# Decoder block on one core: the stage between the out products and the routed experts, by token tiles

## The reference, cut to what matters

```python
x = x + merged @ w_out[i]
h2 = rmsnorm(x, g_ffn[i]).reshape(T, D)
idx, wts = route(h2, w_router[i], router_bias[i])        # sigmoid scores, best 4 of 8 groups, best 8 of 64 experts
moe = routed_experts(h2, idx, wts, w_exp_gate[i], w_exp_up[i], w_exp_down[i]) \
    + swiglu(h2, w_sh_gate[i], w_sh_up[i], w_sh_down[i])  # shared expert, 256 wide
x = x + moe.reshape(B, S, D)
ple_gate = jax.nn.sigmoid(rmsnorm(x, g_ple[i]) @ w_ple_gate[i])
x = x + ple_gate * rmsnorm(p[i] @ w_ple_proj[i], g_ple_post[i])
```

## Time and profile before

| | us |
|---|---|
| median of three runs | 1049.26 (1048.88 to 1050.40) |
| the profiled execution | 1053.37 |
| its span, first to last instruction | 1051.5 |
| TensorE busy | 970.8 (92%) |
| VectorE busy | 290.6 (28%) |
| ScalarE busy | 161.7 (15%) |
| mean granted clock of TensorE | 0.968 of 2.4 GHz |
| first routed up product begins | 397.0 |

### The profile page before, as it was taken

The page is one execution under the profiler, slowest core; times in us unless marked ns, Lnnn a source line. Parts: engine busy times, 40 slices in busy tenths (PEclk is TensorE's granted clock), DMA queues, the critical chain, the costliest instruction groups (busy, mean ns, idle before and its releaser), DMA issues.

```text
span 1051.5 us, 14841 instructions
## 1 busy us (share of the span) xinstructions
PE 970.8 (92%) x6019; PEld 412.9 (39%) x6019; DVE 290.6 (28%) x672; ACT 161.7 (15%) x301; POOL 167.7 (16%) x324
## 2 busy tenths in 40 slices
PE   6999999999999899999999999999987889786598
PEld 4554554444344344333433333333332333232243
DVE  3322642003211564333333111111110101010677
ACT  2002230150000101111111111111110211120021
POOL 4245000000000010222222222222212121201000
PEclk9999999999999899999999999999998989998699
DMA  9351211221231917999999999999999999997972
GB/s 337 123 160 42 79 41 49 71 80 40 75 137 41 373 47 287 368 402 416 410 402 407 400 397 418 417 405 365 423 421 421 421 420 419 420 397 288 374 264 80
DMA packets 74787, 292.79 MB, mean 278 GB/s; under 512 B 8196, under 2 KB 26272, under 8 KB 49760
## 3 DMA queue, kind: packets, MB, share of 16 engines
q1 hardware_dynamic: 61968, 255.90, 62.0%
q0 software_dynamic: 12176, 33.86, 8.3%
q10 hardware_dynamic: 576, 2.10, 0.5%
HBM read 275.57 MB, written 25.69 MB: 286 GB/s over the span
## 4 chain that ended last, share of the span: by engine, by line
PE 74%; DMA 20%; DVE 2%; SPq 1%; issue 1%; ACT 1%; POOL 0%; POOLq 0%; DVEq 0%
PE ps L1713 22%; DMA ring<-in_w_exp_up 18%; PE ps L1441 11%; PE ps L1741 8%; PE ps L1826 5%; PE ps L1543 5%; PE ps L1362 3%; PE ps L1425 3%; PE ps L1385 3%; PE ps L1528 3%; PE ps L1526 3%; PE ps L1589 2%; PE ps L1391 1%; PE ps L1574 1%; PE ps L1724 1%
## 5 line engine op out<-in xcount | busy, mean ns | idle before, releaser
L1713 PE MATMUL ps<-ring,gates 128*32 128x512 f32 x2624 | 301.9, 614 | 33.9 <-DMA ring<-in_w_exp_up 32.4
L1713 PEld LDWEIGHTS ps<-ring,gates 128*32 128x32 f32 x2624 | 93.2, 113 | 236.8 <-issue 235.0
L1741 PE MATMUL ps<-ring,poolbuf 128*32 128x512 f32 x1312 | 149.3, 595 | 1.7 <-ACT actT L776 0.9
L1212 DVE COPY poolbuf<-ps 128x256 f32<-128x256 f32 x41 | 17.4, 424 | 416.3 <-PE ps L1724 416.3
L1441 PE MATMUL ps<-actT,ring 128*128 128x512 f32 x256 | 112.3, 596 | 0.0
L603 POOL TENSOR_TENSOR tickets<-cst 128x1 f32<-128x1 f32 x79 | 14.8, 188 | 397.4 <-ACT actT L776 391.8
L1741 PEld LDWEIGHTS ps<-ring,poolbuf 128*32 128x32 f32 x1312 | 38.9, 110 | 88.6 <-issue 87.3
L1441 PEld LDWEIGHTS ps<-actT,ring 128*128 128x128 f32 x256 | 48.0, 190 | 59.5 <-issue 59.4
L776 ACT ACTIVATE actT<-ps,qT 128x1024 f32<-128x1024 f32 x41 | 45.6, 1113 | 149.2 <-PE ps L1741 149.2
L1362 PE MATMUL ps<-cst,rows 128*128 128x128 f32 x392 | 54.9, 288 | 11.3 <-DMA cst<-in_constants 9.0
L768 ACT ACTIVATE poolbuf<-ps 128x256 f32<-128x256 f32 x41 | 15.7, 384 | 286.0 <-PE ps L1713 286.0
(11 more groups left out here) (227 smaller groups left out, 830.8 us busy)
## 6 DMA issues: line engine op xcount, KB each, us to landing
ring<-in_w_exp_gate SPq DMA_DIRECT2D x64, 1024.0 KB, 13.7
ring<-in_w_exp_up SPq DMA_DIRECT2D x64, 1024.0 KB, 16.7
ring<-in_w_exp_down SPq DMA_DIRECT2D x64, 1024.0 KB, 16.8
ring<-accumulator SPq DMA_DIRECT2D x16, 1024.0 KB, 14.1
ring<-in_w_gate SPq DMA_DIRECT2D x8, 1024.0 KB, 11.5
ring<-in_w_in SPq DMA_DIRECT2D x5, 1024.0 KB, 12.7
ring<-in_w_out SPq DMA_DIRECT2D x4, 1024.0 KB, 5.2
ring<-in_w_ple_gate SPq DMA_DIRECT2D x4, 1024.0 KB, 16.2
```

What stands on the lines that cost most here:

```text
L1713: last = mm(bank(2 + k)[part, :], hgT[k][:, q, part], pair_view(EXPERT_SLOT[js[c]])[:, q], start=(q == 0), stop=(q == KD - 1))
L1741: last = mm(bank(6 + half)[part, :], eactT[r % 2][:, q, part], w[:, q, half * 512:(half + 1) * 512], start=(q == 0), stop=(q == 1))
```

## The change

All stages from the residual addition to the lists are done tile by tile and placed between the out products.

- `out_proj` is called by halves and quarters; for tile 0, half 0, product k waits only for `merged_ready` k+1.
- The rows are no longer scaled before they are transposed. `second_T(i, half)` transposes `xrow` itself, and VectorE multiplies by g_ffn while it copies (g_ffn as a column comes with `vecs`, one more small load on GpSimd's queue). Rows for DRAM are made by `gained_rows` (VectorE, times g_ffn) and a scaled copy on ScalarE. The square of the last tile goes to PSUM.
- The router runs per tile, eight products of 64 columns with the tile as the stationary operand; the reciprocal root is a scale of the sigmoid. The copy and the four transposes of the logits are gone. The router's, and the shared gate's and up's, weights are loaded with channels in the other order (rows of 256 B and 1 KiB instead of 2 KiB and 8 KiB per partition).
- `select(i)` makes the whole selection of a tile, and `rank(i)` its ranks. Sorting uses transposes of the masked ranks and scores instead of products that give transposed ranks.
- The shared up product is four token tiles instead of four blocks of features. Tiles 2 and 3 stand behind `up(0)`. Its activation by features is got by two jobs of transposes (`shared_T`) at steps 22 and 23.
- SyncE loads some of the first experts earlier (expert 1's gate, experts 2's and 3's down weights before the out products end), and the gate and up weights of expert 3 and the projection weights `w_ple` later, behind the first load of group 1.

The diff, cut to what the prediction speaks of. SyncE first:

```diff
             sp.wait_ge(mix_ps, NG)
             load_in(0, 0)
             load_down(0, 0)
-            sp.wait_ge(x1_ready, 2 * NT)
+            load_part(1, 1, 0)
+            load_down(2, 2)
+            load_down(3, 3)
+            sp.wait_ge(x1_ps, 2 * NT - 1)
+            load_part(1, 1, 1)
+            load_down(1, 1)
+            sp.wait_ge(x1_ps, 2 * NT)
+            load_in(2, 2)
             sp.dma_start(gpost, t["g_ple_post"].broadcast_to([P, D])).then_inc(late_loaded, 16)
-            for e in (1, 2):
-                load_in(e, e)
-                load_down(e, e)
-            load_down(3, 3)
-            sp.wait_ge(logit_ps, 1)
+            sp.wait_ge(logit_ps, NT)
             sp.wait_ge(pT_ps, 2)
             sp.dma_start(w_shd, t["w_sh_down"][0].rearrange("(j p) n -> p j n", p=P)).then_inc(late_loaded, 16)
-            sp.wait_ge(shared_ps, 2)
-            load_in(3, 3)
-            sp.wait_ge(sorted_ps, 1)
-            for j in range(2):
-                sp.dma_start(w_ple[j], t["w_ple_proj"][0][j * P:(j + 1) * P, :]).then_inc(late_loaded, 16)
             sp.wait_ge(order_ready, 1)
+            def load_last_fixed():
+                sp.wait_ge(shared_ps, NT)
+                load_in(3, 3)
+                sp.wait_ge(h2_stored, 16 * NT)
+                for j in range(2):
+                    sp.dma_start(w_ple[j], t["w_ple_proj"][0][j * P:(j + 1) * P, :]).then_inc(late_loaded, 16)
...
                 if e:
                     in_used(step)
                     load_in(pos, e[0])
+                    if g == 1:
+                        load_last_fixed()
```

ScalarE, from the first square on:

```diff
+            second_square(0)
+            second_rows(0)
+            second_square(1)
+            second_rows(1)
+            expert_scores(0)
+            second_square(2)
+            second_rows(2)
+            expert_scores(1)
+            expert_scores(2)
+            second_square(3)
+            expert_scores(3)
+            second_rows(3)
+            act.wait_ge(maskedT_ps, 1)
+            nc.scalar.activation(rankT, bank(6)[0:NE, :], ACT.Copy).then_inc(maskedT_ready, 1)
+            nc.scalar.activation(scT, bank(3)[0:NE, :], ACT.Copy).then_inc(maskedT_ready, 1)
```

VectorE, from the first residual on:

```diff
+            residual(0, 0)
+            residual(0, 1)
+            gained_rows(0, 0)
+            gained_rows(0, 1)
+            residual(1, 0)
+            residual(1, 1)
+            second_T(0, 0)
+            second_T(0, 1)
+            gained_rows(1, 0)
+            gained_rows(1, 1)
+            residual(2, 0)
+            select(0)
+            residual(2, 1)
+            second_T(1, 0)
+            second_T(1, 1)
+            for j in range(2):
+                dve.wait_ge(pT_ps, j + 1)
+                nc.vector.tensor_copy(pT[:, j, :], bank(6 + j)).then_inc(pT_ready, 1)
+            gained_rows(2, 0)
+            gained_rows(2, 1)
+            second_T(2, 0)
+            second_T(2, 1)
+            select(1)
+            residual(3, 0)
+            select(2)
+            second_T(3, 0)
+            ranks(0, 3)
+            places(0, rank3[:, :, 0:FIXED], ((0, 3),))
+            residual(3, 1)
+            gained_rows(3, 0)
+            second_T(3, 1)
+            gained_rows(3, 1)
+            select(3)
+            weights_masked(0, 3)
+            ranks(3, 4)
+            places(0, rank3[:, :, 0:FIXED], ((3, 4),))
+            weights_masked(3, 4)
```

TensorE, from the first out product to behind the first routed up product:

```diff
+            out_proj(0, 0)
+            out_proj(0, 1)
+            out_proj(1, 0)
+            out_proj(1, 1)
+            second_T(0, 0)
+            second_T(0, 1)
+            out_proj(2, 0)
+            router(0, 0)
+            router(0, 1)
+            out_proj(2, 1)
+            second_T(1, 0)
+            second_T(1, 1)
             pe.wait_ge(p_loaded, 16)
...
+            out_proj(3, 0, 0, 4)
+            router(1, 0)
+            router(1, 1)
+            second_T(2, 0)
+            second_T(2, 1)
+            out_proj(3, 0, 4, 8)
+            router(2, 0)
+            router(2, 1)
+            out_proj(3, 1, 0, 4)
+            second_T(3, 0)
+            out_proj(3, 1, 4, 6)
+            for i in range(NT - 1):
+                rank(i)
+            out_proj(3, 1, 6, 8)
+            router(3, 0)
+            second_T(3, 1)
             pe.wait_ge(pT_ready, 2)
+            shared_up(0, 0, 1)
+            router(3, 1)
+            shared_up(0, 1, 6)
+            rank(3)
...
+            shared_up(0, 6, 7)
...
             for s in range(steps_of(0)):
-                last = list_rows(0, bank(1)[:, 288 + s * TCOL:288 + (s + 1) * TCOL], s)
+                last = list_rows(0, bank(5)[:, 328 + s * TCOL:328 + (s + 1) * TCOL], s)
             last.then_inc(list_ps, 1)
-            shared_up(1, 0)
-            pe.wait_ge(sort_ready, 1)
+            shared_up(0, 7, 8)
+            pe.wait_ge(masked_ready, 2)
...
+            pe.wait_ge(maskedT_ready, 2)
+            shared_up(1, 0, 2)
             for i in range(NT):
                 mm(bank(6)[:, i * NE:(i + 1) * NE], rankT[:, i * P:(i + 1) * P], perm, start=True, stop=True)
...
+            shared_up(1, 2, 4)
...
             rows_T(0)
+            shared_up(1, 4, 8)
             for r in range(STEPS):
                 up(r)
                 if r:
                     acts_T(r - 1)
                 if r + 1 < STEPS:
                     rows_T(r + 1)
+                if r == 0:
+                    pe.wait_ge(shared_act, 1)
+                    shared_up(2, 0, KD)
+                    pe.wait_ge(tokw_ready, 1)
+                    shared_up(3, 0, KD)
                 if 1 <= r < NGROUP:
                     lists(r)
```

More of the change, by code:

```diff
@@ L1042, in _, with residual @@
-            gm = masked[:, 0:G3]
-            gix = masked[:, G3:G3 + NEG].bitcast(U32)
-            gixf = masked[:, 2 * G3:2 * G3 + NEG]
-            eq = masked[:, 3 * G3:4 * G3]
-            for i in range(NT):
-                gi = gsum[:, i * NEG:(i + 1) * NEG]
-                link(nc.vector.max(gsort, gi))
-                link(nc.vector.max_index(gix, gsort, gi))
+            def residual(i, half):
+                dve.wait_ge(x1_ps, 2 * i + half + 1)
+                xs = xrow[:, i, half * 512:(half + 1) * 512]
+                nc.vector.tensor_tensor(xs, xs, bank(half), ALU.add).then_inc(x1_ready, 1)
@@ L1538, in out_proj @@
                         loaded(f"out{2 * half + 1}")
+                        pe.wait_ge(gate_copied, 2 * KD)
                     else:
                         pe.wait_ge(x1_ready, 2 * i - 1 + half)
[L1541 to L1545 removed]
@@ L1547, in second_T @@
-            def second_T(i):
-                pe.wait_ge(h2_ready, i + 1)
-                if i >= 2:
-                    pe.wait_ge(h2T_ready, 2 * i - 2)
-                strided_T(rows[:, i, :], i, 2 + 2 * (i % 2), P, h2T_ps)
-            out_proj(0)
-            out_proj(1)
-            out_proj(2)
-            second_T(0)
-            out_proj(3)
-            second_T(1)
+                w = pair_view(DENSE_SLOT[DENSE_AT[f"out{2 * half}"]])
+                for k in range(k0, k1):
+                    if i == 0 and half == 0:
+                        pe.wait_ge(merged_ready, k + 1)
+                    last = mm(bank(half), gates[:, k, i * P:(i + 1) * P], w[:, k], start=(k == 0),
+                              stop=(k == KD - 1))
@@ new lines, in out_proj, with second_T @@
+                if k1 == KD:
+                    last.then_inc(x1_ps, 1)
+            def second_T(i, half):
+                pe.wait_ge(x1_ready, 2 * i + half + 1)
+                if i:
+                    pe.wait_ge(h2T_ready, 2 * i - 1 + half)
+                for k in range(4):
+                    last = nc.tensor.transpose(bank(2 + half)[:, k * P:(k + 1) * P],
+                                               xrow[:, i, (4 * half + k) * P:(4 * half + k + 1) * P], ident)
+                last.then_inc(h2T_ps, 1)
@@ new lines, in router @@
+            def router(i, half):
+                if half == 0:
+                    if i == 0:
+                        pe.wait_ge(rw_loaded, 16)
+                    elif i == 1:
+                        pe.wait_ge(pT_ready, 2)
+                    else:
+                        pe.wait_ge(scores_ready, i - 1)
+                pe.wait_ge(h2T_ready, 2 * i + half + 1)
+                for k in range(4 * half, 4 * half + 4):
+                    last = mm(bank(LOGIT_BANK[i])[:, 0:NE], actT[:, k, i * P:(i + 1) * P], rw[:, k, :],
+                              start=(k == 0), stop=(k == KD - 1))
+                if half == 1:
+                    last.then_inc(logit_ps, 1)
@@ new lines, in rank, with shared_up @@
+            def rank(i):
+                pe.wait_ge(sel_ready, i + 1)
+                at = bank(5)[:, i * NE:(i + 1) * NE]
+                for q in range(i):
+                    mm(at, oneT[:, :], selb[:, q * NE:(q + 1) * NE], start=(q == 0), stop=False)
+                mm(at, triT[:, :], selb[:, i * NE:(i + 1) * NE], start=(i == 0), stop=True).then_inc(rank_ps, 1)
+            def shared_up(i, k0, k1):
```

(9 more changed lines are left out.)

424 lines of the change are left out of this document (196 added, 228 removed).

## The result

| | before | after |
|---|---|---|
| median | 1049.77 us (four runs) | 1036.15 us (four runs, 1035.55 to 1036.73) |
| ratio after to before | | 0.9876, 95% interval 0.9860 to 0.9893 |
| profiled execution | 1053.37 us | 1035.55 us |
| its span | 1051.5 us | 1033.7 us |
| mean granted clock of TensorE | 0.968 | 0.979 |

13.6 us faster; 14.0 were forecast. The lines of the new kernel that matter: L1603 out products, L1613 transposes of a tile, L1627 router, L1636 and L1637 ranks, L1646 shared up, L1421 transposes of gathered rows, L1812 routed up, L1840 routed down, and on ScalarE L780 and L781, the two copies ahead of the permutation. In the kernels of the experiments the same lines can stand up to three numbers off.

What follows compares the result with a forecast made beforehand. Bound: TensorE with holes until the third up product ends, then weight transfers at a full queue. -4.1 (start), -13.3 (other holes), +2.3 (new holes) give -15.1; plus 1.1 for small pieces, -14.0: 1049.3 to 1035.3 us, range 1030 to 1045.

Steps and rivals of the forecast that it cites:

- The quantity: End of the third up product, `up(2)`: a microsecond won ahead of it shortens the whole; forecast 410.5 against 425.6 us.
- the first release: Rival: the full transfer stretch begins with `up(0)`, whose start moves 27.8 us; gain 20 to 28, about 1025 us; chance 0.06.
- nothing coming through: Rival: the end of the weights doesn't hang on when they were first asked for; time stays at 1049 us; chance 0.06.
- the full stretch: DMA share 0.97 to 1.02 from about 426 to 950 us, claimed to begin when `up(2)` ends and frees weight slots.
- Holes, not work: TensorE from 281.5 to 425.6 us: work stays about 127 us, so the gain is holes only, at most 17 us.
- The start: Start of out 0: products wait only for their merged blocks, removing a 2.1 us wait and the slow clock behind it: -4.1 us.
- the walk: Step-by-step timing of the new order on TensorE from the out products to `up(2)`, ending at 410.5 us, 15.1 us sooner.
- +2.3 for the new ones: New TensorE holes in the new order ahead of `up(0)`, set against -4.1 at the start and -13.3 for other holes.
- The store: Tile 3's rows sent by ScalarE at 351.4, taking 6.4 us to 357.8; gathered rows land at 363.8, arriving with TensorE.
- No slack, no stall: VectorE's queue from 332.8 holds 12.5 to 13.2 us, done at 346.0, just when the last residual is ready to go.
- The handed-over wait: Rival: VectorE, tile 3's store or the copies before the permutation run late; gain 5 to 11 us, about 1041; chance 0.20.
- Slow clock: Rival: TensorE's clock stays at its lower level from 309 to 369 us; up to +15 us, 1064; chance 0.06 (above 1051).

## Why the prediction was right, point by point

**The quantity.** That the time follows the end of the third up product was right: 13.9 us of position for 13.6 of time here, 13.5 for 12.9 to 14.8 with work ahead, nothing that can be told from zero with work at steps 32 to 39. The rivals of the first release and of nothing coming through are out. That the full stretch begins when this product ends was not: in the kernel after it begins 16 us sooner. And "wait for an expert's weights, 18.8 us at first and 21.8 us at the last" misreads: those are the times that the transfers took. TensorE's own waits for these weights in the kernel before are 14 with 32.4 us together, the longest 5.2. The conclusion does not hang on it, but how much work can be hidden there does.

**Holes, not work.** Right. The start gave its 4.1 (2.1 wait, 2.0 clock) in the profiles. Each router tile is 1.73 us for 1.8; the last out product ended at 345.8 for 346.0; a selection took 3.94 us (318.78 to 322.72) for 4.0. The allowance of 1.1 us for "the small pieces that the walk prices back to back" was not needed there at all.

**Two slips in the walk.** From 363.9, `rows_T(0)` at 0.9 and four shared products at 3.44 end at 368.2 and not at 369.2. The hole ahead of the permutation, from 357.4 to 358.7, is 1.3 and not 0.8 (measured: 0.8). So the sum's "+2.3 for the new ones" and -13.3 have no rows behind them: the new holes that the walk itself has are 1.3 by its words and 1.8 by its positions. Added up rightly, the walk gives 409.5 and -16.1.

**The store.** The one term that was mis-sized: "I take 6.4", and it took 9.0 beside gpost, expert 2's gate and up and the shared down weights. Against it stood 0.8 us up to the store's start (350.6 for 351.4), most of it since GpSimd's two steps on the last tile took 0.19 and 0.90 us and not the 1.17 and 0.55 of the earlier trace rows. The gathered rows came at 365.6 for 363.8, TensorE waited 1.4 us for them, and the first up product began at 370.25 for 369.2. The allowance, put down for another reason, and the microsecond added too much covered this. With the walk's -15.1 alone the forecast would have been 1.5 us too low, with a right addition 2.5. That 14.0 met 13.6 so closely is luck; that it lay within 3 us is the mechanism.

**Slack on VectorE.** "No slack, no stall" was right for the kernel as it is: `places` ended at 345.8, and the last residual began at 345.87. "If a select cost 1 us more, tile 3 would be 2 us late; TensorE has no filler there" was half right: 1.4 us late, of which 0.6 to 0.9 reached the third up product, because another chain, store and gather, was already later than TensorE.

**The handed-over wait.** The rival was there in small: 2.2 us of new waits. It becomes real, 6 us, when the first experts' loads stay behind the last out product. I had looked for it in the store; it sits mostly in the gather.

**Slow clock.** Not seen in any window between 281 and 412 of the kernel after. What the Trainium skill reports of one kernel, "TensorE: Matmul & The Clock Gate" on depth-cycling of PSUM queues, that frequent short idle times make the clock swing, didn't come about here: about twenty changes of product kind and waits of 0.8 and 1.4 us left it at 1.00. What it fell behind in these stages were single waits of 2.1, 2.3 and 6.2 us, and in the kernel before the stretch of waits of 0.9 to 1.7 us with only transposes between them. This makes no rule: in the routed part of the kernel after, the up product behind a wait of 3.7 us took 7.07 us, its time at full clock, and those behind waits of 3.2 to 3.5 us took 8.7.

**The router's short runs.** 256 KB in runs of 256 B landed 8.0 us after issue where runs of 2 KiB took 7.2, with 24 us to spare. The Trainium skill, "DMA: Bandwidth & Descriptors", Specifications, wants at least 512 B for full rate; no run here isolates this, since other loads beside the router's changed too, and the 0.8 us can be theirs.

## What to carry to other kernels

When one resource is full for most of the span, look for a position on the busiest engine that the time follows, and test it from both sides. Here work ahead of it cost in full, moves among what lies ahead (the shared tiles) were worth nothing by themselves, and work far behind it was free as long as it fitted into the waits there. Read those from the waits of the engine: the chain shows how long a transfer took, which can be many times what anybody waited for it. When an order by tiles closes the waits, look next at the longest chain of transfers beside it (here a store and a gather), and clear the queues of what isn't wanted yet. The wait of some 2 us ahead of the out products cost nearly twice its length in position, because the products behind it ran at half clock.

## What the runs showed of the hardware that was not expected

A store of 512 KB issued from ScalarE's queue landed 3.8 us after issue with 2 MiB issued 5 us before it, 9.0 with gpost and the shared down weights (1.5 MiB) besides, and 9.4 with 8.5 MiB asked for in the 5 us before it: it is not served behind all that was asked for before it (the shared down weights, asked for 0.3 us before the store, landed 25.4 us after issue). A gather of rows beside full queues took 9.0 us for 4.7. The same 128x1 `tensor_scalar` of GpSimd took 0.19, 0.69 or 1.17 us from one tile to the next (0.19, 0.19, 1.17, 1.17 before; 0.69, 0.69, 0.19, 0.19 after). And two executions of one kernel differ by 3 to 4 us in what follows the third up product, more than many an edit ahead of it is worth; the position of that product repeated within 0.3 us in both pairs of profiles and tells such edits apart where the time can't.
